# Two expert loads brought forward in halves, one pair's weights by halves, and one subtraction moved, in a two-block sequence model

## Chip, core and metric

The program runs on one core of a Trainium2 chip. Its engines are TensorE (PE; PEld is its weight load), VectorE (DVE), ScalarE (ACT), GpSimd (POOL) and SyncE (SP), which issues the DMAs. Times are microseconds on the device, from the first to the last instruction of one execution and a little around it; less is better.

## What is computed

The input x has 256 tokens of 1024 features. The first block is a gated mixer (a linear recurrence and a spatial gating unit) and a mixture of 32 experts, each token going to two; the second block has two hybrid layers. Cut to what the change touches:

```python
# first block: spatial gating, then the experts
y_sgu = spatial_gating(gelu(u), gelu(v), ...)
mix = concat([y_lru, y_sgu]) @ w_out
x = x + g1 * mix
h = rmsnorm(x, norm2_g) * (1 + sc2) + sh2
# for every expert e, on the tokens that chose it, weighted:
y = (silu(h @ w1[e]) * (h @ w3[e])) @ w2[e]        # 1024x512, 1024x512, 512x1024
x = x + g2 * y
# second block, for each of two layers
proj = rmsnorm(x) @ w_in                            # 1024 x 4360
(aq, ak, av, ag, bq, bk, bv, bg, cq, ck, cv, co, cg, ci, cf) = split(proj)
ya = attention(aq, ak, av) * silu(ag)               # 8 heads, softmax with a linear bias
yb = head_norm(retention(rotate(bq), rotate(bk), bv)) * silu(bg)   # scores * decay
yc = head_norm(mlstm(cq, ck, cv, ci, cf) * sigmoid(co)) * silu(cg)
x = x + concat([ya, yb, yc]) @ w_out
out = rmsnorm(x, final_norm_w)
```

All inputs are float32, 290 MB of them weights that are each read once.

## The kernel before

The program is written by hand for each engine, with semaphores; nothing is scheduled by a tool, and the order on an engine is that of the code.

**The weights' stream.** `stream` lists 114 loads of 2 MB (128 partitions x 4096 floats), all issued by SyncE in order: 0 to 17 for the first block's mixer and modulation, 18 to 113 for the experts. The experts go by 16 pairs, six loads each: two w1, two w3, two w2; pair n begins with load 18 + 6n (`first_load`). Eight slots hold them, six in the tile `ring`, two in `more`; `slot_of` gives each load's slot, `place(n)` its tile, and `slot_free(n)` makes SyncE wait until the load that held the slot before is used up (`freed`). Load 18 takes slot 0 from load 11, used up when VectorE has summed it (semaphore `s_fma`, line 358). Load 26, the first w3 of pair 1, takes slot 0 from load 18. Load 30 takes slot 7 from load 22, the first w2 of pair 0, used up by the last products of that pair (line 1035). A load in `HALVED` is issued as two halves (k 0 to 3, k 4 to 7) that land on semaphores of their own, and waits for the halves of its slot apart: before, the first w_in load, 26, 27 and the last four. `arrival(n, half)` is what a user waits for.

**The experts on TensorE** (`experts_pe`). For a pair n, two experts side by side: w1 products into bank 3 (line 1003, 16 steps of two products; it waits for the arrivals at k = 0 and k = 4), w3 products into bank 4 (also line 1003), the gathering of tokens for the next quartet of experts (line 935; it ends in the tile `xg`, half q % 2 for quartet q), small transposes, the scatter of the pair before (line 975, in the last pair between w1 and w3), and the w2 products (line 1035). VectorE multiplies the gate (1122), ScalarE copies (1075). `xg` lies over the place of `scr`, which the mixer uses until the gating product of the spatial unit (line 772, semaphore `s_sgu`, 8 when done).

**The second block.** Each layer's weights come in units of 1 MB into `raw`. For float32 precision with faster products they are split in two tiles (`halves`): ScalarE copies the high part (`high`, line 1324), VectorE subtracts it to get the low part (`low`, line 1332), in pieces of half a unit, in the order of the list PIECES. For the attention's values (units 10 and 11, `by_token`, TensorE line 1455) that order is 10 first, 11 first, 10 second, 11 second; `low(l, u, i)` makes all pieces up to piece i of unit u. TensorE begins the value products with the first pieces of both units. Around them, on TensorE: the retention's scores (`r_scores`, 1564), the mean of the mLSTM's output (`norm_mean`, 1588), two steps of values, the retention's output (`r_out`, 1577), the variance (`norm_var`, 1592), the rest of the values. On VectorE: `low(l, 10, 0)`, `m_gate` (2036), `r_decay` for heads 0 and 1 (lines 2043 and 2044, the scores times the decay, from which `r_out` reads), the further low pieces, `scaled` (1943), `norm_center` (2069), `r_decay` 2 and 3. ScalarE squares the centered values (1790) for the variance and takes its root (1794).

Of the kernel before, what the change touches and what calls it, by code (L numbers as in the profile page):

```python
# [58 lines left out]
def build(nc, p, out):  # L59
    pe, act, dve, pool, sp = nc.tensor, nc.scalar, nc.vector, nc.gpsimd, nc.sync  # L60
    with ExitStack() as ctx:
# [3 lines left out]
        def sem(name):  # L65
            return ctx.enter_context(nc.semaphore(name))
# [49 lines left out]
        def v3(a, j):  # L116
            return a.rearrange("p (j n) -> p j n", j=j)
# [28 lines left out]
        turns_of = [[n for n in range(len(stream)) if slot_of[n] == i] for i in range(NS)]  # L146


        HALVED = (W_IN[0], 26, 27, len(stream) - 4, len(stream) - 3, len(stream) - 2, len(stream) - 1)
        s_ring = [sem(f"s_ring{i}") for i in range(NS)]  # L150
        s_ahead = [sem(f"s_ahead{i}") for i in range(2)]
        s_more = {i: sem(f"s_more{i}") for i in sorted({slot_of[n] for n in HALVED})}

        def ahead(U):

            return U % NU in (4, 5)
# [9 lines left out]
        def unit_signal(U):  # L166
            return s_ahead[U % NU - 4] if ahead(U) else s_ring[U % 4]

        def unit_arrival(U):
            if ahead(U):  # L170
                return unit_signal(U), 16 * (U // NU + 1)
            return unit_signal(U), 16 * (len(turns_of[U % 4]) + sum(not ahead(x) for x in range(U % 4, U + 1, 4)))

        def arrival(n, half=0):
            i = slot_of[n]
            if half and n in HALVED:
                return s_more[i], 16 * ([m for m in HALVED if slot_of[m] == i].index(n) + 1)
            return s_ring[i], 16 * (turns_of[i].index(n) + 1)


        s_cols, s_x, s_cst, s_late, s_b1, s_out = (sem("s_" + n) for n in ("cols", "x", "cst", "late", "b1", "out"))
# [54 lines left out]
        Gw, oh, pos, w0, w1, w2 = (v3(tables[:, i, :], 2) for i in range(6))  # L236
        Pm, PT = (Pm0, Pm1), (PT0, PT1)
        Pw = [v3(Pw[:, s, :], 2) for s in range(2)]
        xg = [v3(xg[:, s, :], 8) for s in range(2)]
        sg, aT = flat(X1[:, :, :])[:, 0:512], v3(flat(X1[:, :, :])[:, 512:1024], 4)  # L240
        ac = flat(X2[:, :, :])[:, 640:1152]
        weight = [small[:, 216 + s:217 + s] for s in range(2)]
# [14 lines left out]
        def place(n):  # L257
            k, w = stream[n].shape[1], stream[n].shape[2]
            slot = ring[:, slot_of[n], :] if slot_of[n] < 6 else more[:, slot_of[n] - 6, :]
            return slot[:, 0:k * w].rearrange("p (k n) -> p k n", k=k)  # L260
# [19 lines left out]
        def slot_free(n, half=1):  # L280

            held = [m for m in turns_of[slot_of[n]] if m < n]
            if held:
                sp.wait_ge(*freed(held[-1], half))
            elif slot_of[n] == 7:
                sp.wait_ge(s_proj, 19)
# [6 lines left out]
        def experts_sp(first, last):  # L293
            for n in range(first, last):
                for m in range(first_load(n), first_load(n) + 6, 2):
                    if m in HALVED:
                        for half in range(2):
                            for x in (m, m + 1):
                                slot_free(x, half)
                                h = slice(4 * half, 4 * half + 4)  # L300
                                sp.dma_start(place(x)[:, h, :], stream[x][:, h, :]).then_inc((s_more if half else s_ring)[slot_of[x]], 16)
                    else:
                        stream_sp(m, m + 2)
# [676 lines left out]
        def experts_pe(first, last):  # L980
            for n in range(first, last):
                q, o = n // 2, 128 * (n % 2)

                for i in range(2):
                    at = [first_load(n) + 2 * i + x for x in range(2)]
                    if i == 0:
                        pe.wait_ge(s_xg0, 2 * q + 1)
                        pe.wait_ge(s_xg1, 2 * q + 1)
                        if n:
                            pe.wait_ge(s_pg, n)  # L990
                            pe.wait_ge(s_pwt, n)
                        else:
                            pe.wait_ge(s_pos, 2)
                    elif n:
                        pe.wait_ge(s_aT, n)
                    for k in range(8):
                        if i == 0 and k == 4:
                            pe.wait_ge(s_xg0, 2 * q + 2)
                            pe.wait_ge(s_xg1, 2 * q + 2)
                        for x in range(2):  # L1000
                            if k % 4 == 0:
                                pe.wait_ge(*arrival(at[x], k // 4))
                            t = pe.matmul(bank[3 + i][64 * x:64 * x + 64, :], xg[q % 2][:, k, o + 64 * x:o + 64 * x + 64],  # L1003
                                          place(at[x])[:, k, :], start=k == 0, stop=k == 7)
                        if k % 4 == 3:
                            t.then_inc(s_up, 1)
                    if i == 0 and n == NP - 1:
                        scatter_pe(n - 1)
# [229 lines left out]
        def second_block():  # L1238
# [700 lines left out]
            def second_dve():  # L1939
# [93 lines left out]
                def m_gate(l):  # L2033
                    dve.wait_ge(s_gs, 4 * l + 1)
                    dve.wait_ge(s_yc, 6 * l + 6)
                    dve.tensor_tensor(yc, yc, co, ALU.mult).then_inc(s_nV, 1)
# [151 lines left out]
                for l in range(2):  # L2188
# [57 lines left out]
                    take(den1, 3)  # L2246
                    low(l, 10, 0)
                    m_gate(l)
                    r_decay(l, 0)
                    r_decay(l, 1)  # L2250
                    low(l, 10)
# [241 lines left out]
```

## Time and profile before

| what | us |
|---|---|
| median of 3 runs (916.18, 917.47, 918.38) | 917.47 |
| the profiled execution | 916.16 |
| its span | 914.8 |
| TensorE busy | 863.6 |
| VectorE busy | 414.1 |
| ScalarE busy | 301.4 |
| share of the chain of waits that is DMA | 26% |

The profile is one execution. The span runs from the first to the last instruction; 1.4 us lie around it. Up to about 140 us the first block's mixer runs, to 592 the experts, then the two layers, each about 154 us. A row of the waits says who waited for whom; a row of the timeline in order of time gives start, length, engine, line, operation, and in brackets the engine's idle time before it and what ended it; a row of a DMA group ends with the time from issue to landing. Engine names with a q are their queues.

### The profile page before, as it was taken

What the parts mean: (1) busy time and instruction counts of PE and PEld (TensorE: products, weight loads), DVE (VectorE), ACT (ScalarE), POOL (GpSimd) and SP (SyncE); (2) the same over time, 40 slices, a digit from 0 to 9 for tenths busy, and PEclk for the clock granted to TensorE, in tenths of its full rate; (3) what the DMA queues carried; (4) which work ended last, traced back from release to release, by engine and by line L of the source; (5) the groups of instructions that cost most, each with busy time, mean ns of one, the idle gap of its engine ahead of it and who ended that gap; (6) DMA issues with size and microseconds to landing.
All of it is one profiled execution on the core that took longest, in us unless ns stands there. A gap on an engine that the chain in (4) does not pass through costs nothing.

```text
span 914.8 us, 12403 instructions
## 1 busy us (share of the span) xinstructions
PE 863.6 (94%) x5152; PEld 561.4 (61%) x5152; DVE 414.1 (45%) x802; ACT 301.4 (33%) x544; POOL 10.3 (1%) x14
## 2 busy tenths in 40 slices
PE   5899999999998989998998899999999999999997
PEld 3568874434444424442444333498968999887997
DVE  3196953111211102101121101289898888888973
ACT  4253142101111101110111111265546676637572
POOL 0001000000000000000000000000100000000000
PEclk9999999999999999999999999989999999999999
DMA  9999989999999999999999999664315445432441
GB/s 376 422 428 426 360 350 427 426 427 428 428 426 428 427 427 428 426 428 427 428 428 426 428 427 421 266 238 168 136 47 190 152 159 194 159 139 92 139 140 47
DMA packets 25546, 291.40 MB, mean 319 GB/s; under 512 B 2832, under 2 KB 3344, under 8 KB 4240
## 3 DMA queue, kind: packets, MB, share of 16 engines
q1 hardware_dynamic: 25488, 290.58, 77.0%
q8 instruction: 42, 0.69, 0.3%
q14 instruction: 16, 0.13, 0.0%
HBM read 289.52 MB, written 1.05 MB: 318 GB/s over the span
## 4 chain that ended last, share of the span: by engine, by line
PE 67%; DMA 26%; DVE 5%; SPq 1%; issue 1%; ACT 1%
PE bank L1431 22%; PE bank L1003 14%; DMA ring<-in_expert_w 13%; DMA more<-in_expert_w 10%; PE bank L1035 7%; PE bank L1455 4%; PE bank L388 3%; DMA ring<-in_ada_w 3%; PE bank L935 2%; DVE X L358 2%; PE bank L975 2%; PE bank L431 2%; PE bank L404 1%; PE bank L1479 1%; PE bank L1605 1%; DVE halves L1332 1%
## 5 line engine op out<-in xcount | busy, mean ns | idle before, releaser
L1003 PE MATMUL bank<-ring,xg 128*64 128x512 f32 x768 | 238.0, 608 | 17.4 <-DMA ring<-in_expert_w 17.4
L1431 PE MATMUL bank<-HH,halves 128*128 128x256 f32 x848 | 165.1, 290 | 0.0
L1003 PEld LDWEIGHTS bank<-ring,xg 128*64 128x64 f32 x768 | 75.1, 140 | 127.4 <-issue 97.0
L1431 PEld LDWEIGHTS bank<-HH,halves 128*128 128x128 f32 x848 | 136.4, 194 | 5.6 <-issue 4.8
L1003 PE MATMUL bank<-more,xg 128*64 128x512 f32 x256 | 116.5, 607 | 7.5 <-DMA more<-in_expert_w 7.5
L1431 PE MATMUL bank<-HL,halves 128*128 128x256 f32 x424 | 120.9, 285 | 0.0
L1122 DVE TENSOR_TENSOR X<-X,bank 128x512 f32<-128x512 f32 x16 | 11.0, 688 | 232.2 <-PE bank L1003 232.2
L1035 PE MATMUL bank<-ring,X 128*64 128x512 f32 x384 | 113.3, 595 | 0.7 <-ACT X L1075 0.7
L1332 DVE TENSOR_TENSOR halves<-raw,halves 128x1024 fp32r<-128x1024 f32 (+1 forms) x84 | 91.8, 1127 | 6.3 <-ACT halves L1324 6.3
L1135 DVE SCALAR_TENSOR_TENSOR ygL<-bank,small,ygH 128x512 fp32r<-128x512 f32 x32 | 24.0, 750 | 133.0 <-ACT ygH L1082 133.0
L1431 PEld LDWEIGHTS bank<-HL,halves 128*128 128x128 f32 x424 | 82.3, 194 | 0.8 <-issue 0.5
L1324 ACT ACTIVATE halves<-raw 128x1024 fp32r<-128x1024 f32 (+1 forms) x84 | 78.3, 978 | 5.1 <-DMA raw<-in_units 5.1
L1003 PEld LDWEIGHTS bank<-more,xg 128*64 128x64 f32 x256 | 35.0, 140 | 57.8 <-issue 45.8
L1035 PEld LDWEIGHTS bank<-ring,X 128*64 128x64 f32 x384 | 34.5, 137 | 50.4 <-issue 48.0
L1082 ACT ACTIVATE ygH<-bank,small 128x512 fp32r<-128x512 f32 x32 | 22.0, 687 | 120.0 <-PE bank L1035 120.0
L1046 ACT ACTIVATE xg<-bank,modc 128x256 f32<-128x256 f32 x32 | 13.5, 472 | 139.3 <-PE bank L935 135.2
L1035 PE MATMUL bank<-more,X 128*64 128x512 f32 x128 | 56.6, 595 | 0.7 <-ACT X L1075 0.7
L1431 PE MATMUL bank<-YH,halves 128*128 128x256 f32 x256 | 46.4, 283 | 0.0
L1063 ACT ACTIVATE X<-bank 128x512 f32<-128x512 f32 x16 | 9.6, 597 | 108.6 <-PE bank L1003 108.6
L1455 PE MATMUL bank<-halves,HH 128*128 128x512 f32 x128 | 41.8, 407 | 2.8 <-DVE halves L1332 2.8
L1431 PEld LDWEIGHTS bank<-YH,halves 128*128 128x128 f32 x256 | 40.1, 192 | 0.0
L1431 PE MATMUL bank<-YL,halves 128*128 128x256 f32 x128 | 36.2, 283 | 0.0
(345 smaller groups left out, 1196.0 us busy)
## 6 DMA issues: line engine op xcount, KB each, us to landing
ring<-in_expert_w SPq DMA_DIRECT2D x68, 2048.0 KB, 26.4
more<-in_expert_w SPq DMA_DIRECT2D x22, 2048.0 KB, 27.1
raw<-in_units SPq DMA_DIRECT2D x38, 1024.0 KB, 4.8
ring<-in_ada_w SPq DMA_DIRECT2D x10, 2048.0 KB, 21.0
ring<-in_expert_w SPq DMA_DIRECT2D x8, 1024.0 KB, 30.5
ring<-in_w_in SPq DMA_DIRECT2D x3, 2048.0 KB, 34.8
more<-in_ada_w SPq DMA_DIRECT2D x2, 2048.0 KB, 28.0
ring<-in_w_out SPq DMA_DIRECT2D x2, 2048.0 KB, 22.1
```

What stands on the lines that cost most here:

```text
L358: dve.scalar_tensor_tensor(a, w[:, k, :], cs[:, k:k + 1], a, ALU.mult, ALU.add).then_inc(s_fma, 1)
L388: t = pe.matmul(ps[:, T * j:T * j + T], w[:, k, 128 * (first + j):128 * (first + j) + 128], rhs[:, k, :], start=k == 0, stop=k == 7)
L431: t = pe.matmul(bank[6 + i][:, :], hT[:, k, 128 * i:128 * i + 128], w[:, k, :], start=k == 0, stop=k == 7)
L935: t = pe.matmul(ps[:, T * k:T * k + T], part(ht[:, i, d:d + 128]), part(Pm[q % 2][:, i, :]), start=j == 0, stop=j == 3)
L1003: t = pe.matmul(bank[3 + i][64 * x:64 * x + 64, :], xg[q % 2][:, k, o + 64 * x:o + 64 * x + 64], place(at[x])[:, k, :], start=k == 0, stop ...
L1035: t = pe.matmul(bank[5 + a][64 * x:64 * x + 64, :], aT[:, f, 64 * x:64 * x + 64], place(at[x])[:, 4 * a + f, :], start=f == 0, stop=f == 3)
L1082: act.activation(part(ygH[:, 512 * a:512 * a + 512]), bank[5 + a][:, :], ACT.Copy, scale=weight[n % 2]).then_inc(s_ygh, 1)
L1135: dve.scalar_tensor_tensor(part(ygL[:, h]), bank[5 + a][:, :], weight[n % 2], ygH[:, h], ALU.mult, ALU.subtract).then_inc(s_ygl, 1)
L1324: act.activation(part(hi), src, ACT.Copy).then_inc(s_hi, 1)
L1332: dve.tensor_tensor(part(lo), src, hi, ALU.subtract).then_inc(s_lo, 1)
L1431: t = pe.matmul(ps[:, T * j:T * j + T], part(x[:, k, 128 * j:128 * j + 128]), part(y[:, k, :]), start=first and a == 0, stop=last and a == ...
L1455: t = pe.matmul(v3(ps[j][:, :], 2), part(x[:, k, 128 * j:128 * j + 128]), part(y), start=k == 0 and a == 0, stop=k == 7 and a == 2, skip_g ...
```

## The change

Three edits. First, the experts' first load (18, called ASIDE) comes in two halves: its first half goes to the second half of `xg`, as soon as `s_sgu` is 8, the other half to its slot as before; and the first half of load 26 (SOONER), whose place in slot 0 is thereby unused, is issued right behind. TensorE reads the first half of 18 from `xg`. Second, the last six loads come by halves, not the last four, so also the last pair's w1. Third, on VectorE the first low piece of unit 11 is made before the decays of heads 0 and 1, not after them.

```diff
-        HALVED = (W_IN[0], 26, 27, len(stream) - 4, len(stream) - 3, len(stream) - 2, len(stream) - 1)
+        HALVED = (W_IN[0], 26, 27) + tuple(range(len(stream) - 6, len(stream)))
...
+        ASIDE, SOONER = 18, 26
+        s_aside, s_sooner = sem("s_aside"), sem("s_sooner")
...
         def arrival(n, half=0):
             i = slot_of[n]
+            if not half and n in (ASIDE, SOONER):
+                return (s_aside if n == ASIDE else s_sooner), 16
...
-        xg = [v3(xg[:, s, :], 8) for s in range(2)]
+        xg, aside = [v3(xg[:, s, :], 8) for s in range(2)], xg[:, 1, :]
...
                 for m in range(first_load(n), first_load(n) + 6, 2):
-                    if m in HALVED:
+                    if m == ASIDE:
+                        sp.wait_ge(s_sgu, 8)
+                        sp.dma_start(v3(aside, 4), stream[m][:, 0:4, :]).then_inc(s_aside, 16)
+                        slot_free(m)
+                        sp.dma_start(place(m)[:, 4:8, :], stream[m][:, 4:8, :]).then_inc(s_ring[slot_of[m]], 16)
+                        sp.dma_start(place(SOONER)[:, 0:4, :], stream[SOONER][:, 0:4, :]).then_inc(s_sooner, 16)
+                        stream_sp(m + 1, m + 2)
+                    elif m in HALVED:
                         for half in range(2):
                             for x in (m, m + 1):
+                                if x == SOONER and not half:
+                                    continue
                                 slot_free(x, half)
...
-                            t = pe.matmul(bank[3 + i][64 * x:64 * x + 64, :], xg[q % 2][:, k, o + 64 * x:o + 64 * x + 64],
-                                          place(at[x])[:, k, :], start=k == 0, stop=k == 7)
+                            w = v3(aside, 4) if at[x] == ASIDE and k < 4 else place(at[x])
+                            t = pe.matmul(bank[3 + i][64 * x:64 * x + 64, :], xg[q % 2][:, k, o + 64 * x:o + 64 * x + 64], w[:, k, :], start=k == 0, stop=k == 7)
...
                     m_gate(l)
+                    low(l, 11, 0)
                     r_decay(l, 0)
```

The other lines of the diff keep the counts of the ring's semaphores in step. Where the order moves, in three places (a row: line, operation, tile written, tiles read, shape, what it waits for; lines of the changed kernel are 6 to 16 higher):

SyncE before, from the last loads of the modulation (in_ada_w) to the experts' load 27; 18 is the first row with in_expert_w1:

```order
L291 DMA ring<-in_ada_w 128x4096 [waits s_proj]
L291 DMA ring<-in_expert_w1 128x4096 [waits s_fma]
L291 DMA more<-in_expert_w1 128x4096 [waits s_fma]
L291 DMA ring<-in_expert_w3 128x4096 [waits s_proj]
L291 DMA ring<-in_expert_w3 128x4096 [waits s_fma]
L291 DMA more<-in_expert_w2 128x4096 [waits s_proj]
L291 DMA ring<-in_expert_w2 128x4096 [waits s_proj]
L291 DMA ring<-in_expert_w1 128x4096 [waits s_mod] x2
L301 DMA ring<-in_expert_w3 128x2048 [waits s_up]
L301 DMA more<-in_expert_w3 128x2048 [waits s_up]
```

SyncE now, the same stretch:

```order
L297 DMA ring<-in_ada_w 128x4096 [waits s_proj]
L304 DMA xg<-in_expert_w1 128x2048 [waits s_sgu]
L306 DMA ring<-in_expert_w1 128x2048 [waits s_fma]
L307 DMA ring<-in_expert_w3 128x2048
L297 DMA more<-in_expert_w1 128x4096 [waits s_fma]
L297 DMA ring<-in_expert_w3 128x4096 [waits s_proj]
L297 DMA ring<-in_expert_w3 128x4096 [waits s_fma]
L297 DMA more<-in_expert_w2 128x4096 [waits s_proj]
L297 DMA ring<-in_expert_w2 128x4096 [waits s_proj]
L297 DMA ring<-in_expert_w1 128x4096 [waits s_mod] x2
L316 DMA more<-in_expert_w3 128x2048 [waits s_up]
L316 DMA ring<-in_expert_w3 128x2048 [waits s_up]
```

Load 18 is two halves, the first to xg behind another semaphore, and load 26's first half has moved from behind the first eight loads to right behind 18.

SyncE before, the last two pairs' loads and the first units of the second block:

```order
L291 DMA ring<-in_expert_w 128x4096 x4
L291 DMA more<-in_expert_w 128x4096
L291 DMA ring<-in_expert_w 128x4096 x2
L301 DMA more<-in_expert_w 128x2048
L301 DMA ring<-in_expert_w 128x2048
L301 DMA more<-in_expert_w 128x2048
L301 DMA ring<-in_expert_w 128x2048 x5
L2364 DMA raw<-in_units 128x2048 x2
```

SyncE now, the same stretch:

```order
L297 DMA ring<-in_expert_w 128x4096 x4
L297 DMA more<-in_expert_w 128x4096
L316 DMA ring<-in_expert_w 128x2048 x4
L316 DMA more<-in_expert_w 128x2048
L316 DMA ring<-in_expert_w 128x2048
L316 DMA more<-in_expert_w 128x2048
L316 DMA ring<-in_expert_w 128x2048 x5
L2380 DMA raw<-in_units 128x2048 x2
```

Two whole loads (108 and 109) have become four halves, the first halves of both ahead of the second ones.

VectorE before, in each layer of the second block, from the mLSTM's output over its gate to the centering (L1332 is `low`, L2043 and L2044 the decays):

```order
L2030 TENSOR_TENSOR scr<-bank,scr 128x256
L1332 TENSOR_TENSOR halves<-raw,halves 128x1024
L2036 TENSOR_TENSOR scr<-scr 128x2x256
L2043 TENSOR_TENSOR X<-bank,late 128x256
L2044 TENSOR_TENSOR X<-bank,late 128x128
L2043 TENSOR_TENSOR X<-bank,late 128x256
L2044 TENSOR_TENSOR X<-bank,late 128x128
L1332 TENSOR_TENSOR halves<-raw,halves 128x1024 x2
L1943 TENSOR_TENSOR scr<-bank,rs 128x512
L1332 TENSOR_TENSOR halves<-raw,halves 128x1024
L2069 TENSOR_TENSOR scr<-scr,bank 128x2x256
```

VectorE now, the same stretch:

```order
L2045 TENSOR_TENSOR scr<-bank,scr 128x256
L1347 TENSOR_TENSOR halves<-raw,halves 128x1024
L2051 TENSOR_TENSOR scr<-scr 128x2x256
L1347 TENSOR_TENSOR halves<-raw,halves 128x1024
L2058 TENSOR_TENSOR X<-bank,late 128x256
L2059 TENSOR_TENSOR X<-bank,late 128x128
L2058 TENSOR_TENSOR X<-bank,late 128x256
L2059 TENSOR_TENSOR X<-bank,late 128x128
L1347 TENSOR_TENSOR halves<-raw,halves 128x1024
L1958 TENSOR_TENSOR scr<-bank,rs 128x512
L1347 TENSOR_TENSOR halves<-raw,halves 128x1024
L2084 TENSOR_TENSOR scr<-scr,bank 128x2x256
```

One of the two subtractions behind the decays now stands ahead of them; the rest keeps its order.

## Rows read from the trace of the kernel before

**Rows 1.** The page: clock by slice, and the chain's shares by engine.

```profile
PEclk9999999999999999999999999989999999999999
...
PE 67%; DMA 26%; DVE 5%; SPq 1%; issue 1%; ACT 1%
```

**Rows 2.** Waits of TensorE, 240 to 570 us: total, times, longest.

```profile
PE bank L1003 <- DMA ring<-in_expert_w: 17.4, 9, 2.7
```

**Rows 3.** Timeline of SyncE's queue: start, length, line, what is loaded.

```profile
99.81 0.33 SPq L291 DMA_DIRECT2D ring<-in_expert_w  x1
107.30 0.33 SPq L291 DMA_DIRECT2D more<-in_expert_w  x1
...
126.13 0.33 SPq L291 DMA_DIRECT2D more<-in_expert_w  x1
...
165.23 0.33 SPq L291 DMA_DIRECT2D more<-in_expert_w  x1
```

**Rows 4.** Windows: busy by engine, clock, DMA share, GB/s last.

```profile
100.00:110.00 10.00, 10.00 (x50) 8.81 (x49) 9.58 (x20) 2.11 (x6) 0.00 (x0) 1.00 0.80 280
...
122.00:130.00 8.00, 8.00 (x67) 7.27 (x69) 1.92 (x10) 2.38 (x6) 0.00 (x0) 1.00 0.57 202
...
164.00:170.00 6.00, 6.00 (x30) 2.01 (x28) 0.75 (x1) 0.69 (x1) 0.00 (x0) 1.00 1.00 423
```

**Rows 5.** Timeline of VectorE: the last gating product.

```profile
93.45 0.42 DVE L772 TENSOR_TENSOR yT<-yT,scr 128x256 f32<-128x256 f32 x1
```

**Rows 6.** DMA issues at 107.30, 126.13 and 165.23: us to landing last.

```profile
more<-in_expert_w SPq DMA_DIRECT2D x1, 2048.0 KB, 7.8
...
more<-in_expert_w SPq DMA_DIRECT2D x1, 2048.0 KB, 8.8
...
more<-in_expert_w SPq DMA_DIRECT2D x1, 2048.0 KB, 9.2
```

**Rows 7.** Chain (start, us, what), and timeline of TensorE, in the last pair.

```profile
535.12 28.91 DMA ring<-in_expert_w
...
561.19 1.02 PE L1003 MATMUL bank<-ring,xg 128*64 128x512 f32 x2
564.08 7.08 PE L1003 MATMUL bank<-ring,xg 128*64 128x512 f32 x30 [1.87 <-DMA ring<-in_expert_w]
...
573.26 7.04 PE bank L1003 x32
...
582.41 7.09 PE L1035 MATMUL bank<-ring,X 128*64 128x512 f32 x32 [0.69 <-ACT X L1075]
```

**Rows 8.** Half loads issued at 541.99, then two at 551.0 and 551.8: landing.

```profile
ring<-in_expert_w SPq DMA_DIRECT2D x1, 1024.0 KB, 32.2
...
DMA to landing us min/median/max: 30.6/31.4/32.3
```

**Rows 9.** Timeline of TensorE at the attention's values, layer 0.

```profile
668.04 0.70 PE L1455 MATMUL bank<-halves,HH 128*128 128x512 f32 x2 [1.39 <-DVE halves L1332]
...
670.94 0.87 PE L1577 MATMUL bank<-X,scr 128*64 128x256 f32 x8
672.07 1.13 PE L1592 MATMUL bank<-scr,late 128*128 128x512 f32 x2 [0.26 <-ACT scr L1790]
```

**Rows 10.** Timeline of VectorE in the same stretch.

```profile
664.12 0.69 DVE L2036 TENSOR_TENSOR scr<-scr 128x512 f32<-128x512 f32 x1
665.61 0.42 DVE L2043 TENSOR_TENSOR X<-bank,late 128x256 f32<-128x256 f32 x1 [0.80 <-PE bank L1564]
...
666.67 2.35 DVE L1332 TENSOR_TENSOR halves<-raw,halves 128x1024 fp32r<-128x1024 f32 x2
...
670.68 0.68 DVE L2069 TENSOR_TENSOR scr<-scr,bank 128x512 f32<-128x512 f32 x1
```

**Rows 11.** Timeline of ScalarE in the same stretch.

```profile
671.39 0.63 ACT L1790 ACTIVATE scr<-scr 128x512 f32<-128x512 f32 x1 [11.86 <-DVE scr L2069]
```

**Rows 12.** One window, as in rows 4: the clock is the third number from the end.

```profile
606.00:614.00 8.00, 8.00 (x42) 7.82 (x42) 4.84 (x12) 4.57 (x6) 0.00 (x0) 0.57 0.16 69
```

More of the change, by code:

```diff
@@ L171, in unit_arrival @@
                 return unit_signal(U), 16 * (U // NU + 1)
-            return unit_signal(U), 16 * (len(turns_of[U % 4]) + sum(not ahead(x) for x in range(U % 4, U + 1, 4)))
+            return unit_signal(U), 16 * (len([n for n in turns_of[U % 4] if n != SOONER]) + sum(not ahead(x) for x in range(U % 4, U + 1, 4)))
         def arrival(n, half=0):
             i = slot_of[n]
+            if not half and n in (ASIDE, SOONER):
+                return (s_aside if n == ASIDE else s_sooner), 16
             if half and n in HALVED:
                 return s_more[i], 16 * ([m for m in HALVED if slot_of[m] == i].index(n) + 1)
-            return s_ring[i], 16 * (turns_of[i].index(n) + 1)
+            return s_ring[i], 16 * (len([m for m in turns_of[i] if m <= n and m != SOONER]))
         s_cols, s_x, s_cst, s_late, s_b1, s_out = (sem("s_" + n) for n in ("cols", "x", "cst", "late", "b1", "out"))
```

## Prediction

> **What bounds the kernel now.** I read the page's summary of the chain first: TensorE carries 67% of it, transfers 26%, everything else 7% [rows 1]. So an edit pays only where it takes idle time out of TensorE or lets transfers land earlier while TensorE waits for them. The kernel has two such places. In the expert stage TensorE waits for weights between 240 and 570 us, 17.4 us of it for the loads named ring, in nine waits [rows 2]; these loads pass through one queue that is full there. In the second block TensorE hardly waits: 1.39 and 0.26 us beside each layer's attention values [rows 9]. The issues of SyncE, the DMA rates by window and the time from issue to landing tell why the queue runs dry early on; VectorE's list in order of time tells of the 1.39 us.
>
> **A. The first expert load in two parts, and half of load 26 early.** Before, load 18 is issued at 99.81, as soon as its slot is free, and 19 at 107.30 [rows 3]. The window 100 to 110 moves 280 GB/s, against 423 in a full stretch: 10 x (1 - 280/423) = 3.4 us of transfer time lost. In 122 to 130, where load 22 waits for a slot until 126.13, it is 8 x (1 - 202/423) = 4.2 us [rows 3, 4]. Now half of load 18 (1.05 MB, 1.05/423 = 2.5 us of queue) waits only for VectorE's last gating product, done at 93.45 + 0.42 = 93.87 [rows 5], and goes to xg. The other half and the first half of load 26 follow at 99.8. Loads 19 to 25 keep their issue times, since their slots come free as before. So at 126 the DMAs are ahead by the half of load 26, 2.5 us, and the dry spell before 107.30 is mostly filled. SyncE's new wait ends 6 us before the one that stood there anyway, so nothing queued behind it is late. TensorE's new waits are for data that lands near 105 and is read after 135: nothing. xg's second half is written only by the gathering for the second quartet, which TensorE does after it has read the aside half: no new wait.
>
> How much of the 2.5 us lasts? From then on a load is issued when TensorE frees its slot, and TensorE is no earlier. The tight place is load 30, issued at 165.23 [rows 3]: it lands after 9.2 us, while loads that met an empty queue took 7.8 us (issued at 107.30) and 8.8 us (126.13) [rows 6]. So the queue ahead of it costs only 9.2 - 8.8 = 0.4 to 9.2 - 7.8 = 1.4 us; with a queue 2.5 us shorter it lands 0.4 to 1.4 us earlier, and the rest is an idle DMA at 165 to 167, where the rate now is a full 423 GB/s [rows 4]. I take 1.1, nearer to 1.4, because the queue will have been dry for about a microsecond, as at 107.30, and not for over three as before 126.13. The 1.1 us then lasts: the later loads are queued far longer (the last ones 28.91 us [rows 7]), and TensorE's waits of 240 to 570 [rows 2] turn it into time. **A = 1.1 us**, bounds 0.4 and 2.5.
>
> The Trainium skill (DMA: Bandwidth & Descriptors, Anatomy of one DMA) fits a transfer, on its software path, by 2.0 us plus bytes at 436 GB/s, which gives 6.8 us for 2.1 MB. By that page the queue ahead of load 30 would cost 9.2 - 6.8 = 2.4 us, A would be 2.4 and the sum 1.3 us larger; the two landings from an empty queue, 7.8 and 8.8 us on the hardware path, disagree with it, and I go by them.
>
> **B. The last pair's first weights (108, 109) by halves.** TensorE has finished pair 14 and started pair 15 at 561.19, does two products, idles 1.87 us, and goes on at 564.08 when load 109 has landed (535.12 + 28.91 = 564.03) [rows 7]. By halves, the first halves of both are there when load 108 lands whole today, about 4.9 us (2.1/0.423) earlier, at 559.1: before TensorE asks. The first half then runs 561.2 to 564.7 (half of 7.08), the second needs what lands at 564.03, and ends at 568.3 instead of 564.08 + 7.08 = 571.16: 2.9 us. Then other landings come last. The scatter takes 573.26 - 571.16 = 2.1 us, so the w3 products start at 570.4; their second half needs the half load issued at 541.99, which lands 32.2 us later at 574.2 [rows 8]. They end at 574.2 + 3.5 = 577.7 instead of 580.3. The w2 products start at 579.8 instead of 582.41; their first half ends at 583.35, and the second needs the last half load, issued at 551.8 with 32.3 us: 584.1. The end is 584.1 + 3.55 = 587.65 instead of 582.41 + 7.09 = 589.5 [rows 7, 8]. **B = 1.85 us**, and a wait for w2's last half of 0.75 us is what stands there next. If TensorE has to restart like today it may be 1.0; if the last landings move too, 2.9. The extra issues (0.33 us each on SyncE) are hidden by a queue of 28 us. A and B add, because all these landings move by A.
>
> **C. The low half of the attention's second values ahead of the decays.** In layer 0 VectorE ends the gate product at 664.12 + 0.69 = 664.81, idles 0.80 us until TensorE's scores, makes the decays from 665.61 and only then, at 666.67, two low halves; the first of them is the one TensorE waits for. Its value products start at 668.04, after 1.39 us of idling [rows 9, 10]. The copy that the moved subtraction needs was made before 660: ScalarE has been idle for 11.86 us at 671.39 [rows 11]. A low half takes 1.13 us (2.35 for two, overlapping). Moved, it runs 664.81 to 665.94, and TensorE goes on at 668.04 - 1.39 = 666.65 without a wait. The decays start at 665.94, 0.33 late, and end at 667.0; r_out asks for them at 670.94 - 1.39 = 669.55, so they are hidden. What is late next is TensorE's variance product (L1592): it needs ScalarE's square, which needs VectorE's centering (L2069), at 670.68. That comes earlier only by what VectorE stops idling: 0.80 us. TensorE reaches it at 669.55 + 0.87 = 670.42 and waits until about 672.07 - 0.80 + 0.03 = 671.3. So the gain is 0.77, not 1.65, and a wait of 0.9 us for ScalarE takes the place of 1.39 and 0.26. Behind it ScalarE (root) and VectorE follow the square and shift by the same 0.8. Layer 1 repeats these rows with the same numbers (0.80, 1.39, 0.25), so **C = 1.55 us**. Bounds: 0, if another wait takes it back, and 2 x 1.65 = 3.3, if the centering is not what comes next.
>
> **Sum.** 1.1 + 1.85 + 1.55 = 4.5 us. The profiled execution took 916.16 us (span 914.8), so it would become 911.7. It is at the low end of the runs shown, 1.3 under their median of 917.47; from the median the forecast is 913.0.
>
> **The rivals.** (1) *Slot limit takes A back*: load 30 restarts like load 22, 8.8 us, and a landing is set by the slowest of 16 DMA engines. A is 0.4 or less, the time 913.7 to 914.1. For it: the 8.8 us. (2) *The whole half load lasts*: A = 2.5, time 911.6, if the restart is quicker than any seen. (3) *C is taken back or B is only 1*: about 915; for it, that ScalarE's table loads and VectorE's queue are tight behind L1592. (4) *The clock.* In 606 to 614 the granted clock is 0.57 of full, that is 1.2 GHz for most of the stretch, though TensorE is busy throughout [rows 12]; it had been doing products with two output columns (L1479). That costs up to 8 x 0.43 = 3.4 us. Everything there moves 3 us earlier; if the fall stays away, the time is 913.0 - 3.4 = 909.6. The same mechanism gives the slow case: the new 0.9 us wait behind r_out's narrow products could let the clock fall in both layers, at 3.4 us each: 913.0 + 6.8 = 919.8, slower. It decides from two such falls; one gives 916.4, no change. Against it: today's 1.39 us waits at the same place leave the clock row at 9 [rows 1]. (5) *Nothing of A*: if the queue had not been dry; the 280 and 202 GB/s exclude it.
>
> The Trainium skill (TensorE: Matmul & The Clock Gate, Part 1) says that the default state is throttled and that activity releases it. By that rule less idling, as in B and C, can only help; the row of 606 to 614, with TensorE busy for all 8 us, shows that busy time in the profile does not by itself hold the clock.
>
> **How the numbers follow.** Forecast 913.0 (A between 0.8 and 1.8, B and C as worked out): 0.57. Rival 1: 0.14. Rival 2: 0.08. Rival 3: 0.09. Clock stays up, 909.6: 0.05. Clock falls once more, 916.4: 0.04. Twice, 919.8: 0.03. The three runs before spread over 2.2 us, so the range also takes 1 us around the middle cases: 910.3 to 915.4. A measurement of this kernel tells 0.2%, 1.8 us, from no change, so faster means under 915.6: 0.89 (all cases up to 915, less 0.04 for the part of rival 3 that ends above); within: 0.08 (that part and 916.4); slower, over 919.3: 0.03.
>
> **What would show it.** A: the window 100 to 110 near 400 GB/s; load 30 still issued near 165.2 and landing after 7.8 to 8.4 us, with a dip in the rate behind 165; and load 109's landing 1.1 us earlier. B: no idle of 1.87 us in front of L1003 in the last pair, short waits before the second halves of w3 and w2. C: no wait before the value products, and one of about 0.9 us before L1592 in each layer, on ScalarE. I am wrong if load 30 is issued earlier, if the landings at the end do not move, or if the wait at L1592 is gone too.

## The result and the profile after

The changed kernel took 911.37 us, the median of 5 runs (909.71 to 912.64); the kernel before took 916.18, the median of 5 (915.20 to 918.38), in the same comparison. The ratio is 0.9954, 95% interval 0.9940 to 0.9969: 2.8 to 5.5 us less. A second series gave 912.05 us (6 runs) against 915.90 (19 runs), ratio 0.9965 (0.9953 to 0.9977). The forecast was 4.5 us less, 913.0 from a median of 917.47, in a range of 910.3 to 915.4. The kernel before has a median 1.3 us lower in this comparison than in the three runs that the forecast started from; the time is 1.6 us under 913.0, the gain 4.8 us by the medians and 4.2 by the ratio. Both fit the forecast, and the three edits' shares can be told apart only with the experiments below.

The profiled execution of the changed kernel took 912.64 us, with a span of 911.3: 3.5 us under the span of before, 914.8. Its page, clock row and chain, for [rows 1]:

```profile
PEclk9999999999999999999999999999999999999999
...
PE 70%; DMA 20%; DVE 8%; issue 1%; SPq 1%; ACT 1%; DVEq 0%
```

SyncE's queue (start, length, line, what is loaded), for [rows 3]:

```profile
93.76 0.33 SPq L304 DMA_DIRECT2D xg<-in_expert_w  x1
99.67 0.33 SPq L306 DMA_DIRECT2D ring<-in_expert_w  x1
100.04 0.43 SPq L307 DMA_DIRECT2D ring<-in_expert_w  x1
107.16 0.33 SPq L297 DMA_DIRECT2D more<-in_expert_w  x1
125.99 0.33 SPq L297 DMA_DIRECT2D more<-in_expert_w  x1
...
166.23 0.33 SPq L297 DMA_DIRECT2D more<-in_expert_w  x1
```

Windows (busy us of PE, PEld, DVE, ACT, POOL, then granted clock, DMA share, GB/s), for [rows 4] and [rows 12] and three that the result made me look at:

```profile
100.00:110.00 10.00, 10.00 (x50) 8.81 (x49) 9.58 (x20) 2.25 (x7) 0.00 (x0) 1.00 0.99 387
...
134.00:140.00 6.00, 5.21 (x31) 5.07 (x31) 4.90 (x11) 1.18 (x3) 0.00 (x0) 0.72 0.99 426
164.00:170.00 6.00, 6.00 (x32) 2.00 (x30) 1.03 (x2) 0.69 (x1) 0.00 (x0) 1.00 0.87 322
512.00:520.00 8.00, 5.30 (x28) 1.71 (x26) 0.00 (x0) 0.60 (x1) 0.00 (x0) 1.00 1.02 432
544.00:550.00 6.00, 5.47 (x18) 1.74 (x20) 0.00 (x0) 0.00 (x0) 0.00 (x0) 0.72 0.99 418
606.00:614.00 8.00, 8.00 (x54) 7.82 (x55) 5.51 (x15) 4.57 (x6) 0.00 (x0) 0.79 0.13 54
```

The same three additional windows of the kernel before:

```profile
134.00:140.00 6.00, 5.10 (x40) 4.62 (x41) 4.88 (x12) 1.87 (x6) 0.00 (x0) 1.00 1.01 431
512.00:520.00 8.00, 5.45 (x20) 1.84 (x22) 0.00 (x0) 0.48 (x1) 0.00 (x0) 0.79 1.01 426
544.00:550.00 6.00, 6.00 (x29) 2.00 (x30) 0.00 (x0) 0.00 (x0) 0.00 (x0) 1.00 1.02 431
```

Three things stand here. The first dry spell is filled: 387 GB/s where 280 were. The DMA now runs dry at the place that the prediction named, behind 165: 322 GB/s where 423 were. And the granted clock drops to half for part of 134 to 140 and of 544 to 550, where before it was full, which the prediction did not have. Falls as such are not new: before's trace has one in 512 to 520 (0.79), where the changed kernel's clock is full.

The last pair, from the chain of waits (start, us, what), for [rows 7]:

```profile
512.85 31.63 DMA ring<-in_expert_w
544.52 8.79 PE bank L1019 x30
...
556.65 7.02 PE bank L1050 x32
563.66 6.87 PE bank L1019 x32
570.53 2.11 PE bank L990 x16
572.64 7.04 PE bank L1019 x32
581.79 7.56 PE bank L1050 x31
```

L1019 is the line that was L1003, L1050 was L1035, L990 was L975. The idle of 1.87 us in the last pair is gone, but TensorE arrives at that pair at 563.66 instead of 561.19, so the experts end at 581.79 + 7.54 = 589.33 us, a mere 0.17 us ahead of before's 589.50. Read alone, this execution would say that A and B gave nothing.

The attention's values in layer 0, on TensorE, for [rows 9] (L1592 is now the retention's output, which was L1577; the variance, which was L1592, is L1607):

```profile
662.30 1.59 PE L1579 MATMUL bank<-scr 32*128 32x256 f32 x32
...
667.64 0.87 PE L1592 MATMUL bank<-X,scr 128*64 128x256 f32 x8
669.49 1.13 PE L1607 MATMUL bank<-scr,late 128*128 128x512 f32 x2 [0.98 <-ACT scr L1805]
```

Before, the row of the retention's scores (L1564, now L1579), which leads this stretch, was:

```profile
664.00 1.59 PE L1564 MATMUL bank<-scr 32*128 32x256 f32 x32
```

On VectorE now, for [rows 10]:

```profile
663.03 1.22 DVE L1347 TENSOR_TENSOR halves<-raw,halves 128x1024 fp32r<-128x1024 f32 x1
664.17 0.42 DVE L2058 TENSOR_TENSOR X<-bank,late 128x256 f32<-128x256 f32 x1
...
668.10 0.68 DVE L2084 TENSOR_TENSOR scr<-scr,bank 128x512 f32<-128x512 f32 x1
```

No wait is left before the value products. VectorE no longer idles between the gate product and the decays, and TensorE waits 0.98 us for ScalarE's square. Of 1.39 + 0.26 = 1.65 us of waits 0.98 remain. The difference, 0.67 us, is not yet the gain, since a wait is counted from the shown end of the products ahead of it, and without a wait the next products start before that end. The gain is read between two starts: from the scores to the variance it was 672.07 - 664.00 = 8.07 us and is now 669.49 - 662.30 = 7.19. That is 0.88 us per layer, 1.76 for both; layer 1 has 8.08 and 7.19.

So the 3.5 us of this pair of spans are 0.17 us before the experts' end, 1.76 us of C, and most of the rest a shorter clock fall: in 606 to 614 the clock is 0.79, where it was 0.57. Its worth shows in the traces without C that the experiments below left, from the experts' end to the end of the span: 325.3 us at 0.57 (before and b_alone), 323.8 and 324.1 at 0.79 (a_alone, omit24), 1.2 to 1.5 us less. The total fits, but its parts are not those that the prediction put into it.

### The profile page after: what moved, and what is told of

Its sections match the earlier page's. It is cut to its first block, busy times and chain, and to the rows that moved or that the text cites. A ratio compares the mean times of both kernels' runs of the same rounds, so it can differ in the third digit from the quotient of the medians.

```text
span 911.3 us, 12406 instructions
## 1 busy us (share of the span) xinstructions
PE 863.8 (95%) x5152; PEld 562.3 (62%) x5152; DVE 414.0 (45%) x802; ACT 301.4 (33%) x544; POOL 10.3 (1%) x14
## 3 DMA queue, kind: packets, MB, share of 16 engines
HBM read 289.52 MB, written 1.05 MB: 319 GB/s over the span
## 4 chain that ended last, share of the span: by engine, by line
PE 70%; DMA 20%; DVE 8%; issue 1%; SPq 1%; ACT 1%; DVEq 0%
PE bank L1446 20%; PE bank L1019 18%; DMA ring<-in_expert_w 17%; PE bank L1050 9%; PE bank L1470 4%; PE bank L403 3%; DMA ring<-in_ada_w 3%; PE bank L990 2%; PE bank L950 2%; DVE X L373 2%; PE bank L446 2%; DVE halves L1347 1%; PE bank L419 1%; DVE scr L2042 1%; PE bank L1620 1%
## 5 line engine op out<-in xcount | busy, mean ns | idle before, releaser
L1019 PE MATMUL bank<-ring,xg 128*64 128x512 f32 x760 | 234.6, 610 | 16.0 <-DMA ring<-in_expert_w 16.0
L1019 PEld LDWEIGHTS bank<-ring,xg 128*64 128x64 f32 x760 | 74.4, 140 | 134.6 <-issue 105.3
L1019 PE MATMUL bank<-more,xg 128*64 128x512 f32 x256 | 118.4, 615 | 7.0 <-DMA more<-in_expert_w 6.9
L1050 PE MATMUL bank<-ring,X 128*64 128x512 f32 x384 | 113.8, 595 | 0.7 <-ACT X L1090 0.7
L1050 PEld LDWEIGHTS bank<-ring,X 128*64 128x64 f32 x384 | 34.9, 137 | 50.5 <-issue 47.8
L1019 PEld LDWEIGHTS bank<-more,xg 128*64 128x64 f32 x256 | 35.4, 142 | 46.7 <-issue 36.0
L1050 PE MATMUL bank<-more,X 128*64 128x512 f32 x128 | 56.6, 595 | 0.7 <-ACT X L1090 0.7
```

The source lines that it names most:

```text
L1050: t = pe.matmul(bank[5 + a][64 * x:64 * x + 64, :], aT[:, f, 64 * x:64 * x + 64], place(at[x])[:, 4 * a + f, :], start=f == 0, stop=f == 3)
```

## The experiments

Each series is timed against runs of the kernel before beside it. In the traces I look at two rows: the issue of load 30, and the end of the last w2 products. Their difference takes out what delays TensorE ahead of load 30.

**Each edit alone.** A alone is the changed kernel with `HALVED` and the line in the second block as before; the others are:

```diff
b_alone, against the kernel before
-        HALVED = (W_IN[0], 26, 27, len(stream) - 4, len(stream) - 3, len(stream) - 2, len(stream) - 1)
+        HALVED = (W_IN[0], 26, 27) + tuple(range(len(stream) - 6, len(stream)))
c_alone, against the kernel before
                     m_gate(l)
+                    low(l, 11, 0)
                     r_decay(l, 0)
```

> The kernel before with edit A alone (load 18 in two halves, the first aside in xg, and the first half of load 26 early). Theory S (slot limit): the half load ahead is cut at load 30, whose slot comes free at 165.2; the rate in 164 to 170 dips from 423 GB/s to 300 to 400, and the time falls by 0.4 to 1.4 us. Theory W (the whole half load lasts): no dip, 2.4 us less. Theory N (nothing lasts, since later landings are set by the slowest DMA engine and by when TensorE frees slots): within 0.4 us of before. The window 100 to 110 rises to near 390 GB/s in all three.

> The kernel before with edit B alone (the last pair's first weights by halves). Forecast theory: no idle of 1.87 us before the last pair's first products, which start at about 561.2 and end 2.9 us earlier; the last half loads then come last and 1.85 us remain. Rival: TensorE gets to the last pair late in many executions (in the profiled one of the changed kernel at 563.7, after a fall of the clock to 1.2 GHz at 545), and then the whole load would have landed anyway: 0.2 to 1 us remain.

> The kernel before with edit C alone (the first low piece of unit 11 ahead of the decays). Forecast theory: the centering is next, so a wait of 0.9 to 1.0 us before L1592 takes the place of 1.39 and 0.26 us, in both layers: 1.3 to 1.55 us less. Rival (the square is not what comes next): 3.3 us less and no wait. Rival (given back later in the layer): 0.

Measured (12 runs each, before 915.77): A alone 914.88, ratio 0.9994 (0.9985 to 1.0004); B alone 914.53, 0.9991 (0.9976 to 1.0005); C alone 914.52, 0.9984 (0.9973 to 0.9994). That is 0.5, 0.8 and 1.5 us by the ratios; only C's interval excludes no change. A alone, the window of load 30:

```profile
164.00:170.00 6.00, 6.00 (x30) 2.01 (x28) 1.24 (x2) 0.69 (x1) 0.00 (x0) 1.00 0.85 314
```

The dip is there with A alone, and no dip as deep with B alone (366 GB/s) or C alone (360). C alone, waits of TensorE in the second block (total, times, longest):

```profile
PE bank L1592 <- ACT scr L1790: 2.0, 2, 1.0
```

That is the forecast exchange of waits, one us in each layer (0.9 expected). And C alone, which still loads 108 and 109 whole, has no idle time in the last pair, because TensorE comes there late, at 567.17, when load 109 has landed (issued at 536.4, landed after 29.9 us, at 566.3):

```profile
546.72 10.11 PE bank L1003 x30
...
560.15 7.02 PE bank L1035 x32
567.17 6.87 PE bank L1003 x32
```

Pair 14's products of 546.72 take 10.11 us there, at a mean clock of 0.67 in 544 to 550; at full clock they take 7.09 (below). In such an execution B has little to remove.

**Is A limited at load 30?** Two kernels leave out the same 1.05 MB of one expert's weights, the first half of load 24 or of load 62 (so these outputs lack that part). Load 24 lies ahead of the tight place, load 62 behind it.

```diff
omit24, against the kernel before (omit62: n == 62)
-                sp.dma_start(place(n), stream[n]).then_inc(s_ring[slot_of[n]], 16)
+                h = slice(4, 8) if n == 24 else slice(0, stream[n].shape[1])
+                sp.dma_start(place(n)[:, h, :], stream[n][:, h, :]).then_inc(s_ring[slot_of[n]], 16)
```

> The kernel before, but of load 24 (first w1 of pair 1, issued at 131.5) only the second half is loaded; the first half keeps what its slot held. 1.05 MB less to move ahead of load 30, the same relief as edit A gives, without its other parts. Slot-limit theory: load 30 is issued at 165 to 166 as before, the rate dips in 164 to 170 as in A alone (314 GB/s there), and the time falls like A's, by 0.4 to 1.2 us. If instead a lighter queue pays fully, 2.4 us.

> The kernel before, but of load 62 (first w3 of pair 7, issued at about 267) only the second half is loaded. The same 1.05 MB less, but behind the tight place, where loads are queued for 25 us and more. Slot-limit theory: no dip at 164 to 170, the later loads all land 2.4 us earlier, and the time falls by 1.8 to 2.4 us, clearly more than with load 24. If the gain is lost at the end of the experts (TensorE late for the last pair) and not at load 30, both omissions give the same small gain.

Measured: leaving out half of load 24 gives 915.32 us (11 runs), ratio 0.9993 (0.9984 to 1.0003), 0.6 us; leaving out half of load 62 gives 913.09 (7 runs), 0.9976 (0.9963 to 0.9989), 2.2 us. The 2.5 us of queue are worth nearly all of their length behind load 30 and a quarter of it ahead, though the two intervals, 0 to 1.5 us and 1.0 to 3.4 us less, still touch. The window of load 30 with half of load 24 left out shows the same dip as A:

```profile
164.00:170.00 6.00, 6.00 (x30) 2.01 (x28) 1.50 (x2) 0.88 (x2) 0.00 (x0) 1.00 0.89 319
```

With half of load 62 left out it is 360 GB/s. The trace says it more sharply than the times. Load 109 lands 398.8 us after the issue of load 30 in before (564.03 - 165.23) and 399.6 in c_alone; with half of load 24 left out it is 397.5, and with edit A, in a_alone and no_b, 397.5 and 397.6. So the same 2.5 us of queue, by two quite different edits, come through load 30 as the same 1.3 to 2.1 us. That is the slot limit. With half of load 62 left out the experts' end comes 587.48 - 166.60 = 420.9 us after load 30's issue, 3.4 less than before's 424.3 and more than the 2.5 us of queue; the excess of that one trace is not explained.

**Each edit taken out of the whole.** no_a has B and C, no_b has A and C, no_c has A and B; after_again is the changed kernel unaltered, timed with no_b and no_c. no_a was timed in another series, with omit24 and omit62.

```diff
no_b, against the changed kernel
-        HALVED = (W_IN[0], 26, 27) + tuple(range(len(stream) - 6, len(stream)))
+        HALVED = (W_IN[0], 26, 27, len(stream) - 4, len(stream) - 3, len(stream) - 2, len(stream) - 1)
no_c, against the changed kernel
                     m_gate(l)
-                    low(l, 11, 0)
                     r_decay(l, 0)
```

> The changed kernel without edit A (B and C only). Forecast theory: 1.1 us (0.4 to 1.4) above the changed kernel, 3.3 us below before, about 912.4. If A gives nothing: as the changed kernel, 911.4. If A and B help each other (the last pair's first weights pay only when its loads land early), 913 or more.

> The changed kernel without edit B (A and C only). Forecast theory: 1.85 us above the changed kernel. Rival (B pays only where TensorE is in time for the last pair, and alone it gave 0.8 us): 0.8 to 1.2 us above it. If A pays only through B's halves, no_b is no better than C alone, 1.25 to 1.5 us under before.

> The changed kernel without edit C (A and B only). 1.3 us above the changed kernel (0.67 us of waiting per layer), the waits of 1.39 and 0.26 us back in both layers. Nothing in C touches the experts, so this should be the steadiest of the three.

> The changed kernel once more, beside the two kernels that leave one edit out, on the same chip: 911 to 912, ratio to before 0.9954 as measured, if the sum of the three stands.

| edits | kernel | us | ratio (95%) |
|---|---|---|---|
| B, C | no_a | 913.39 | 0.9971 (0.9955 to 0.9986) |
| A, C | no_b | 912.73 | 0.9972 (0.9960 to 0.9984) |
| A, B | no_c | 913.15 | 0.9973 (0.9961 to 0.9985) |
| A, B, C | after_again | 912.05 | 0.9965 (0.9953 to 0.9977) |

Taking one edit out costs 0.5 to 0.7 us by these ratios, and each ratio has 1.1 to 1.4 us on either side; from the first series' 0.9954 it costs 1.6 to 1.7. With the singles: A 0.5 to 1.6 us, B 0.6 to 1.7, C 0.7 to 1.7. What the times show beyond their intervals is that C alone gives something (its single) and that A and B together do (no_c); of A and of B by themselves they don't show it. The traces are sharper. no_b, on TensorE, shows the wait that B removes:

```profile
564.31 7.08 PE L1019 MATMUL bank<-ring,xg 128*64 128x512 f32 x30 [1.29 <-DMA ring<-in_expert_w]
```

and its chain goes on to `PE bank L1050` from 582.64 for 7.11 us, the end at 589.75. The chain of no_c:

```profile
544.70 7.09 PE bank L1019 x30
...
562.14 6.87 PE bank L1019 x32
569.01 2.11 PE bank L990 x16
571.12 7.34 PE bank L1019 x32
...
580.57 7.84 PE bank L1050 x32
```

Here the clock is full in 544 to 550. The w2 products take 7.84 us instead of 7.11: the wait of 0.73 us for the last half load, forecast as 0.75. The w3 products wait 0.3 us for theirs (7.34 against 7.04).

From such rows, the issue of load 30, the experts' end, and the difference (C lies behind this end and is left out of the first column):

| edits | kernel | load 30 issued | end | difference | clock at 544 to 550 |
|---|---|---|---|---|---|
| none | before | 165.23 | 589.50 | 424.3 | 1.00 |
| A | a_alone | 166.44 | 589.46 | 423.0 | 1.00 |
| A | no_b | 166.68 | 589.75 | 423.1 | 1.00 |
| A, B | no_c | 166.86 | 588.41 | 421.6 | 1.00 |
| A, B | center (below) | 166.07 | 587.69 | 421.6 | 1.00 |
| A, B | after_again | 165.78 | 588.04 | 422.3 | 0.73 |
| A, B | after | 166.23 | 589.33 | 423.1 | 0.72 |
| B | b_alone | 166.66 | 590.09 | 423.4 | 0.72 |
| B | no_a | 167.44 | 591.36 | 423.9 | 0.77 |
| none | c_alone | 166.67 | 592.41 | 425.7 | 0.67 |

With a full clock in 544 to 550, A is 424.3 - 423.05 = 1.2 us and B is 423.05 - 421.6 = 1.45. With the fall, A and B together leave 1.2 to 2.0 instead of 2.7. No row is free of falls: those with 1.00 here have 0.79 in 512 to 520 instead. For B this does no harm, since a_alone, no_b, no_c and center all have 0.79 in the same four windows between load 30 and the experts' end (276 to 284, 336 to 344, 424 to 432, 512 to 520). Before's trace has 364 to 372 in place of 336 to 344, so A is less well matched. The row without an edit rests on one trace with a full clock there; with half of load 24 left out it is 582.82 + 7.11 - 166.93 = 423.0, as with A.

**What is next after C.** The prediction said that the wait at L1607 stays because the centering on VectorE is what ScalarE's square needs. So bring the centering of heads 0 and 1 forward, to right behind their decays:

```diff
center, against the changed kernel, in each layer
                     r_decay(l, 1)
+                    norm_center(l, 0)
                     low(l, 10)
...
-                    norm_center(l, 0)
```

> The changed kernel with the centering (norm_center of the mLSTM's output) moved too, right behind the decays of heads 0 and 1, ahead of the other low pieces. If the centering behind VectorE's subtractions is what the remaining 0.98 us wait before L1592 is for, the wait goes in both layers and the time is 1.9 to 2.0 us under the changed kernel's, about 909.4; TensorE has the square at about 668.5, ahead of 669. If it is ScalarE's own queue or another product of VectorE that is late next (the low pieces for the fifth step of the values), a new wait before L1455 or L1620 shows and the gain is under 1 us.

Measured: 910.19 us (6 runs), ratio 0.9938 (0.9923 to 0.9952), the best kernel of this study, 1.2 us under the first series of the changed kernel and 1.9 under the second. Its TensorE in layer 0:

```profile
662.61 1.59 PE L1579 MATMUL bank<-scr 32*128 32x256 f32 x32
...
667.95 0.87 PE L1592 MATMUL bank<-X,scr 128*64 128x256 f32 x8
668.75 1.12 PE L1607 MATMUL bank<-scr,late 128*128 128x512 f32 x2
```

L1607 follows 0.80 us behind L1592's start, where it was 669.49 - 667.64 = 1.85. The wait is gone, in both layers. From the scores to the variance the starts are now 6.14 and 6.13 us apart instead of 7.19: 1.05 us per layer, 2.1 for both, where 1.9 to 2.0 were expected.

**More halves?** On top of center, the last twelve loads by halves (`range(len(stream) - 12, len(stream))`).

> The changed kernel with the centering early (910.19 us) and the last twelve loads by halves, not the last six, so all of pair 14 too. Theory L (TensorE is late for the last pair where the clock fell in pair 14, so B pays only in part): TensorE gets through pair 14 earlier, is free before the last pair's first halves land, and the end of the experts is set by the last half load in more executions: 0.5 to 1.5 us less. Rival (the last half load already sets the end, since B): no change within 0.3 us.

Measured: 910.84 us (6 runs), ratio 0.9941 (0.9925 to 0.9957), no better than center. Its chain:

```profile
548.61 28.20 DMA ring<-in_expert_w
576.86 3.66 PE bank L1019 x14
...
582.62 7.85 PE bank L1050 x32
```

The second half of the w3 products waits for a landing at 576.81, and the w2 products last 7.85 us again, with the wait for the last half load in them. Where landings set the end, TensorE's being early is no use. The difference as in the table is 582.62 + 7.85 - 166.96 = 423.5, 1.9 more than center's, also with a full clock in 544 to 550; that the added halves themselves make the landings later is possible, and one trace doesn't show it.

## Why the prediction was right, point by point

**What bounds the kernel**: as said. In the traces each of the three places gave something, and the kernel with half of load 62 left out shows that the expert stage behind load 30 turns queue time into time.

**A, 1.1 us**: 1.2 by the traces with a full clock in 544 to 550, 0.5 to 1.6 by the times. The mechanism holds: 387 GB/s in 100 to 110, the dip behind 165, and the other loads' issues unmoved (107.16 and 125.99, against 107.30 and 126.13). The lower end, rival 1 (0.4 or less), fits the series of A alone best and the traces worst, and the times don't exclude it. Rival 2, the whole 2.5 us, is out: the same amount left out ahead of load 30 gave 0.6 us, with an interval up to 1.5.

Three signs of "What would show it" did not come as written. Load 30 was issued near 166.2, not 165.2. It landed after 9.6 us in the changed kernel's trace and 8.9 in after_again, not after 7.8 to 8.4; over the traces this landing scatters from 7.8 to 9.6 us with A (median of seven 8.7) and from 8.7 to 9.9 without (median of five, omit24 left aside, 9.2), too widely to measure A by it. The 0.4 and 1.4 us of the prediction are differences of single landings (9.2, 8.8 and 7.8 us) within this scatter, so that 1.1 came near is in part luck. And load 109's landing did not move on the clock of the trace: 535.75 + 28.23 = 563.98 in A alone, where it was 564.03, and the last half load of the changed kernel's first trace landed at 558.0 + 27.6 = 585.6, where it was 584.1. The prediction's condition for being wrong, "if the landings at the end do not move", is met as it is written. In a_alone, no_b and omit24 they move only when counted from the issue of load 30, by 398.8 - 397.5 = 1.3 us or more, as said at omit24, because load 30 itself was 1.2 us later. That delay is not A's. From the issue of load 19 to that of load 30 are 57.9 us in each of the three traces without the fall of the clock in 134 to 140, and 59.1 to 59.4 us in each of the ten with it, whichever the edits.

The Trainium skill (DMA: Bandwidth & Descriptors, Anatomy of one DMA) has for its software path a fit that gives, as an estimate, 6.8 us for a 2.1 MB load. No landing of load 30 was as quick with the dip in front of it: 7.8 us in no_b, 8.7 in a_alone, 9.6 in the changed kernel, on the hardware queue.

**B, 1.85 us**: the term that was too large. The chain of events was right: the idle of 1.87 us goes, 0.3 us are waited for w3's last half and 0.73 for w2's, and the last half load sets the end. With a full clock in 544 to 550 it is 1.45 us. The term rested on one trace of before, in which TensorE came to the last pair at 561.19, 2.8 us ahead of the landing at 564.03. That distance is not a constant of the kernel. In four of the five executions with a fall at 545 TensorE arrives there at 563.66 (after), 564.85, 566.13 and 567.17, and in after_again at 562.81, when the whole load would be there or nearly so; B then has little to remove. The times give 0.6 to 1.7 us, not clear of nothing. I had bounded the landings from both sides (1.0 and 2.9) and never the consumer's arrival.

**C, 1.55 us**: 1.76 by the traces, 1.5 by C alone. The traces agree closely here: from the scores' start to the variance's it is 8.07 or 8.08 us in the six traces without C, 7.18 or 7.19 in the five with it, in both layers. The stretch from the experts' end to the end of the span, at a clock of 0.79 in 606 to 614, says the same less exactly: 323.8 and 324.1 us without C, 321.9 to 322.2 with it (after, no_a, no_b). The forecast gain was 0.77 us per layer and is 0.88. VectorE's idle of 0.80 us was the right cause: the centering starts 668.10 - 662.30 = 5.80 us behind the scores instead of 670.68 - 664.00 = 6.68, and the 0.08 us more than 0.80 are the overlap of one row with the next, which an idle time counted from a row's end leaves out. The wait at the variance is 0.98 us where I had 0.9, and so no loss, since TensorE comes there earlier than I had reckoned. `center` shows that the centering was indeed next. Both edits together take 8.07 - 6.14 = 1.93 us per layer, 3.9 us, which is above the bound of 3.3 that I had put: the sum of the counted waits was no bound.

**Sum, 4.5 us**: 1.2 + 1.45 + 1.76 = 4.4 from the traces, with a full clock in 544 to 550, 4.2 and 3.2 from the two timed series. The sum fits better than its parts: B came out 0.4 us under its term and C 0.2 over. Rival 3, "C is taken back or B is only 1", describes the executions with the fall, by another cause than it names.

**The clock, rival 4**, was aimed at the right quantity and the wrong place. No new fall shows up behind the variance's wait: the granted clock in windows over 669 to 676 and 820 to 832 is 1.00 throughout. The fall at 606 is there or shorter whether or not the edits are: 0.79 with A alone, 0.57 with B alone and with center, 1.00 with no_c. Its price was too high: without C the stretch from the experts' end to the end of the span is 325.3 us at 0.57 and 323.0 and 323.1 at 1.00 (omit62, no_c), 2.2 us and not 3.4. In the traces the falls that decide are at 136 and 545. I had said of before's row only that TensorE was busy while the clock was low, and did not ask whether another execution would have its falls in the same places.

## What to carry to other kernels

A prefetch that is brought forward is worth only what lasts to the next issue that waits for a slot: find that issue, compare its landing time with one from an empty queue, and take the difference, over several traces where there are any (single landings of load 30 scattered by up to 1.8 us here). Halving a load pays by the consumer's idle time in front of it, so bound the consumer's arrival as well as the landing; after that the last landing sets the end, and further halves gave nothing here. Where the work behind a removed wait has its own next dependency on the same engine, only the idle time of that engine is gained, and moving that dependency too can double the gain: 0.88 us per layer became 1.93, and center took 5.7 us (0.0062 x 916) where the change took 3.2 to 4.2. Measure such a gain between two starts, not by adding and subtracting waits, and count an event from one that the edit can't move: the distances of 8.07 and 7.19 us repeat to 0.01 us, where six to twelve runs leave 1 us open.

## What the runs showed of the hardware that I had not expected

**The place of the clock's falls differs between executions.** In 10 of 13 traces the mean granted clock in 134 to 140 is 0.72 to 0.81, that is 1.2 GHz (of 2.4) for part of the stretch; in before's, after_again's and center's it is 1.00. Most of these are traces of different kernels; after and after_again are of one, and they differ in 134 to 140 (0.72 and 1.00) and in 336 to 344 (0.79 and 1.00). In 5 of 13 it is 0.67 to 0.77 in 544 to 550 (in one more 0.89), just after TensorE has waited for a landing and begun pair 14's w1 products: these take 8.79 us in after and 7.09 in no_c. No edit goes with it: the fall shows with B alone, with C alone and with all three, and not in center, which has all three too. What goes with it is the idle time just before: 2.70 to 3.95 us in these six traces, 1.19 to 1.48 in six others, and none in halves12. That is no rule for every place. At 512 to 516 TensorE idles 2.70 us in twelve traces, and the clock then falls in nine (0.79 in 512 to 520) and not in after, b_alone and after_again. The five runs of the first series go with their mean clock: 909.71 us at 0.992, 910.59 and 911.37 at 0.990, 912.41 at 0.988 and 912.64 at 0.986. So the profiled run of the changed kernel was the slowest of its five, and the profiles of before and after were not of the same kind. The Trainium skill (TensorE: Matmul & The Clock Gate, Part 1) has the default state throttled and activity as what releases it; the falls behind the longer waits go with that, and why the same 2.70 us at 512 bring one in nine traces and none in three stays open.

**A fall is not always paid.** In before's trace pair 13's w1 products take 8.48 us instead of some 7.1 under the fall in 512 to 520, and TensorE's next wait for a landing is 1.48 us:

```profile
543.91 2.37 PE L1003 MATMUL bank<-ring,xg 128*64 128x512 f32 x10 [1.48 <-DMA ring<-in_expert_w]
```

In the changed kernel's trace, which has no fall there, that wait is longer by 1.2 us:

```profile
544.52 2.27 PE L1019 MATMUL bank<-ring,xg 128*64 128x512 f32 x6 [2.71 <-DMA ring<-in_expert_w]
```

The wait has taken most of the fall up. The changed kernel's own fall, in 544 to 550, has no such wait behind it, since B has removed the one in the last pair, and 421.6 becomes 422.3 and 423.1. A kernel from which waits are taken is the more open to its clock; that is argued from these rows, and I did not test it.
